# The filling of a softmax block moved behind the turning of its probabilities

## What is computed

```python
for i in range(S // Q_BLOCK):                       # 8 blocks of 128 queries
    s = einsum('bqhmd,bkhmd->bhmqk', q[:, q0:end], k[:, :end]) * scale   # m = 0, 1: two maps
    s = where(rel >= 0, s + bias, -inf)
    p = softmax(s, axis=-1)
    a = p[:, :, 0] - lam * p[:, :, 1]
    out = einsum('bhqk,bkhv->bqhv', a, v[:, :end])
```

## Time and profile before

| | |
|---|---|
| median of three runs | 2386.18 us (2385.57 to 2388.72) |
| the profiled execution | 2384.78 us, span in the trace 2383.0 us |
| TensorE (PE) busy | 2323.8 us, 98% of the span |
| VectorE (DVE) busy | 1611.8 us, 68% |
| ScalarE (ACT) busy | 990.7 us, 42% |
| GpSimd (POOL) busy | 298.8 us, 13% |
| chain that ended last | PE 87%, DVE 5%, DMA 2%, ACT 1% |

### The profile page before, as it was taken

The page is one execution under the profiler, slowest core; times in us unless marked ns, Lnnn a source line. Parts: engine busy times, 40 slices in busy tenths (PEclk is TensorE's granted clock), DMA queues, the critical chain, the costliest instruction groups (busy, mean ns, idle before and its releaser), DMA issues.

```text
span 2383.0 us, 30592 instructions
## 1 busy us (share of the span) xinstructions
PE 2323.8 (98%) x11354; PEld 1873.2 (79%) x11354; DVE 1611.8 (68%) x2740; ACT 990.7 (42%) x1891; POOL 298.8 (13%) x388
## 2 busy tenths in 40 slices
PE   7989999999999999999989999999999999999997
PEld 5778777788788888888778887777888888888886
DVE  6755677767877777576762556776687777655766
ACT  6422455544333233344753125555443333324454
POOL 0256400011000000220120110000200000003001
PEclk9999999999999999999999999999999999999999
DMA  8767501133454555662331111102324554227434
GB/s 306 254 240 225 164 18 35 55 107 92 156 171 151 196 171 150 181 207 95 127 122 45 39 34 45 28 27 80 115 71 168 186 198 173 80 71 240 145 104 153
DMA packets 216019, 311.29 MB, mean 131 GB/s; under 512 B 13207, under 2 KB 151368, under 8 KB 212928
## 3 DMA queue, kind: packets, MB, share of 16 engines
q1 hardware_dynamic: 182884, 188.31, 24.8%
q0 software_dynamic: 32528, 120.62, 15.1%
q10 hardware_dynamic: 460, 0.40, 0.1%
HBM read 243.48 MB, written 71.02 MB: 132 GB/s over the span
## 4 chain that ended last, share of the span: by engine, by line
PE 87%; DVE 5%; DMA 2%; issue 2%; ACT 1%; POOL 1%; SPq 1%; ACTq 0%; DVEq 0%; POOLq 0%
PE ps L3254 32%; PE ps L3293 15%; PE ps L2750 7%; PE ps L3134 7%; PE ps L2752 7%; PE ps L2751 7%; PE ps L3111 3%; PE ps L3080 3%; PE ps L2863 1%; PE ps L3099 1%; DVE ast L2088 1%; PE ps L2824 1%; PE ps L3062 1%; SPq L767 1%; DMA F<-in_w_down 1%
## 5 line engine op out<-in xcount | busy, mean ns | idle before, releaser
L3254 PE MATMUL ps<-hT,wsp 128*128 128x512 f32 x1440 | 333.5, 389 | 2.6 <-issue 2.6
L3254 PEld LDWEIGHTS ps<-hT,wsp 128*128 128x128 f32 x1440 | 269.9, 188 | 60.0 <-issue 4.0
L2750 PE MATMUL ps<-hT,wsp 128*128 128x512 f32 (+1 forms) x696 | 289.8, 416 | 0.0
L2752 PE MATMUL ps<-hT,wsp 128*128 128x512 f32 (+1 forms) x696 | 272.2, 391 | 0.0
L2751 PE MATMUL ps<-hT,wsp 128*128 128x512 f32 (+1 forms) x696 | 271.3, 390 | 0.0
L3293 PE MATMUL ps<-wsp,asp 128*128 128x512 f32 x1056 | 249.7, 392 | 0.2
L3293 PEld LDWEIGHTS ps<-wsp,asp 128*128 128x128 f32 x1056 | 198.1, 188 | 44.0 <-issue 1.0
L3254 PE MATMUL ps<-tsum,wasp 128*128 128x512 f32 x960 | 226.4, 392 | 0.3 <-DVE wasp L2544 0.3
L3254 PEld LDWEIGHTS ps<-tsum,wasp 128*128 128x128 f32 x960 | 180.2, 188 | 39.9 <-DVE wasp L2544 0.8
L2752 PEld LDWEIGHTS ps<-hT,wsp 128*128 128x128 f32 x696 | 131.5, 189 | 28.8
L2750 PEld LDWEIGHTS ps<-hT,wsp 128*128 128x128 f32 x696 | 131.8, 189 | 27.9 <-issue 7.3
(11 more groups left out here) (327 smaller groups left out, 4280.3 us busy)
## 6 DMA issues: line engine op xcount, KB each, us to landing
raw<-in_w_gate_up SPq DMA_DIRECT2D x48, 512.0 KB, 5.3
F<-in_w_mod SPq DMA_DIRECT2D x48, 512.0 KB, 5.5
raw<-in_w_in SPq DMA_DIRECT2D x45, 512.0 KB
raw<-sums_d SPq DMA_DIRECT2D x88, 256.0 KB, 3.0
F<-in_w_gate_up SPq DMA_DIRECT2D x40, 512.0 KB, 5.7
acts_d<-F POOLq DMA_DIRECT2D x38, 512.0 KB, 6.8
F<-acts_d POOLq DMA_DIRECT2D x76, 256.0 KB, 4.3
raw<-in_w_down SPq DMA_DIRECT2D x66, 256.0 KB, 4.0
```

Of the source, the lines that this page charges most:

```text
L2750: mm(o, a(0), b(0), start=start, stop=False)
L2752: return mm(o, a(1), b(0), start=False, stop=stop)
L3254: last = mm(bank(j, p), block_of(p, z)[:, k * P:k * P + P], times(p, zz, k), start=p < B_A22 and k == 0 and z == 0 and zz == 0, stop=k == ...
```

## The change

The two parts of the filling of a block are put together in one run that stands behind the turning of the block's probabilities (in block 7 ahead of the last tile, as the second part was). The number of steps of each block stays the same. `STEPS` holds one number a block, and the helper functions that find out which pieces and halves fall into a block give the same answer as before. The waits are those of the functions and move with them.

```diff
 EARLY = 4
-STEPS = (((2, 2), (2, 2), (3, 2), (2, 2), (2, 1), (2, 1), (2, 1), (1, 1)),
-         ((2, 2), (2, 2), (3, 2), (2, 2), (2, 2), (2, 2), (2, 2), (2, 1)),
-         ((2, 2), (2, 2), (3, 2), (2, 2), (2, 2), (2, 2), (2, 2), (2, 1)),
-         ((2, 2), (2, 2), (3, 2), (3, 2), (3, 2), (3, 2), (2, 2), (0, 0)))
+STEPS = ((4, 4, 5, 4, 3, 3, 3, 2), (4, 4, 5, 4, 4, 4, 4, 3), (4, 4, 5, 4, 4, 4, 4, 3),
+         (4, 4, 5, 5, 5, 5, 4, 0))
...
-                        a = NT * 16 + steps_before(h, b, 0)
+                        a = NT * 16 + steps_before(h, b)
                         if b:
                             weighted(h, b - 1)
-                        fill(a, a + STEPS[h][b][0])
                         if b == 0 and h:
                             weighted(h - 1, NT - 1)
                         turned(h, b, 0)
                         if b >= 4:
                             turned(h, b, 1)
-                        fill(a + STEPS[h][b][0], a + sum(STEPS[h][b]))
+                        fill(a, a + STEPS[h][b])
                         if h == HEADS - 1 and b == NT - 1:
                             out_first(0)
```

More of the change, by code:

```diff
@@ L120, with steps_before @@
 O_HOME = (2, 3, 0, 1, 6, 4, 5, 7)
-def steps_before(h, b, part):
-    return EARLY + sum(sum(p) for hh in range(h) for p in STEPS[hh]) + sum(
-        sum(p) for p in STEPS[h][:b]) + (STEPS[h][b][0] if part else 0)
+def steps_before(h, b):
+    return EARLY + sum(sum(STEPS[hh]) for hh in range(h)) + sum(STEPS[h][:b])
 def pieces_turned(h, b):
-    a = steps_before(h, b, 0)
-    return [i for i in range(len(PIECES)) if a <= 8 * i + 4 < a + sum(STEPS[h][b])]
+    a = steps_before(h, b)
+    return [i for i in range(len(PIECES)) if a <= 8 * i + 4 < a + STEPS[h][b]]
 def halves_ended(h, b):
-    a = steps_before(h, b, 0)
-    return range(a // 8, (a + sum(STEPS[h][b])) // 8)
+    a = steps_before(h, b)
+    return range(a // 8, (a + STEPS[h][b]) // 8)
 Y_PAIR = (0, 1, 2, 3, 0, 1, 0, 1)
```

## The result

The changed kernel takes 2394.8 us (median; 2394.3 to 2395.91) against 2386.11 us of the kernel before in the same comparison: 8.7 us more, a ratio of 1.0035 with a 95% interval of 1.0023 to 1.0047. The forecast was 2389.2 us with a range up to 2392.0 and no difference that can be measured as the likeliest. It was wrong; the kernel is slower, and by nearly three times the forecast.

What follows compares the result with a forecast made beforehand. The prediction took TensorE, busy 98% of the span, to bound the kernel. First-block waits of 1.65 + 1.39 + 0 gave +3.0 us on the median 2386.18, so 2389.2 us, with a range of 2385.5 to 2392.0.

Steps and rivals of the forecast that it cites:

- T(b) waits for the combination of block b: Every block: turning the probabilities waits for VectorE's scalar_tensor_tensor (line 2222); the first part of filling had covered this.
- T(7) waits in every head: Sign that the prediction is wrong: turning the probabilities of block 7 waits in every head.
- First blocks, 1.65 + 1.39 = 3.04: Head 0, block 0: turning waits for the combination, 1.65 us in layer 0 and 1.39 in layer 1.
- T(4) and T(5) eaten by S(6) and S(7): Head 0 block 4, heads 1 and 2 block 5: turning 0.28 and 0.03 us late, absorbed by later score waits; zero.
- T(1) covered in heads 1 to 3: Block 1, heads 1 to 3: 0.1 us left by old times, but exponentials come some 1.5 us sooner; covered.
- W(7) directly behind S(1), zero: Next head's first block: previous head's last weighted values follow scores directly; zero, bounded by 0.3 us six times, 1.7 us.
- pieces behind T, zero: The 12 pieces formerly turned in the first part of filling go at most 0.7 us later; zero.
- joints, zero: In 62 blocks, 0.08 us saved per second filling run cancels 0.08 lost by turning directly behind weighted values; zero.
- B: Rival: near misses bite in blocks 4, 5 and 7, and the last weighted values pay; +5.8, 2392.0 us; chance 0.17.
- D: Rival: granted clock halves behind first blocks' wait (+9.8, 2396.0) or in runs without filling (+30, 2416); chance 0.06, second way 0.02.
- Rival C: First-block delay partly given back at head 0's later score waits, 1.07 and 0.3 us a layer; +0.3, 2386.5; chance 0.13.
- Rival E: Faster: second filling runs saved, turning behind weighted values free, -2.0; old waits drained, another 4.2; 2380.0 us; chance 0.04.

Runs made afterwards that it cites:

- the step between: Changed kernel with one step of filling put between turned group 0 and group 1 in blocks 4 to 7: 2386.74 us, ratio 1.0006.
- the shorter copy: Changed kernel with ScalarE's two steps of outs turned round, copy out of PSUM first, then the square: 2391.29 us, ratio 1.0020.
- The mirror image: Kernel with blocks 4 to 7 of each head in the changed order, blocks 0 to 3 as before the change: 2393.39 us, ratio 1.0031.

## Why the prediction was wrong, by its own steps

- *"T(b) waits for the combination of block b"*, in the part on what bounds the kernel. This is the step that failed. It holds for group 0. Group 1 has a second input, the free bank, and the whole list of later blocks was worked out with the first input only. Missing term: 9 paid waits of 0.40 us a layer, 7.2 us in both, and 0.16 for block 5 of head 0. The row that named this wait was in the very view of the earlier trace rows, 0.2 us in the one block without filling, and was passed over as small. What shows once, where the cover is missing, is to be paid at each place where the cover is taken away, and at 0.40 us and not at the row's 0.2. One of the prediction's own signs of being wrong came true by this wait: T(7) waits in every head.
- *First blocks, 1.65 + 1.39 = 3.04.* Right mechanism; measured 1.27 and 1.28, in all 2.55. The start behind the end of a VectorE step was taken at 0.14 us and is 0.06 here (275.06 + 0.35 = 275.41, T(0) at 275.47, rows below): 0.16 in both layers. The 0.1 us for each wait that the prediction set beside this price does not show; the start came sooner than by the row, not later. The rest is mostly layer 0's chain, which is not tied to S(1): the combination ended 2.14 us behind the start of S(1) in the trace of before, 1.87 here, and 2.8 to 3.0 in four of the other traces.
- *T(4) and T(5) eaten by S(6) and S(7).* Right about what eats, wrong about what is eaten: T(4) came 0.11 late for its combination and T(5) not at all, this cost nothing, and what S(6) of head 0 (1.07 down to 0.67) and S(7) of heads 1 and 2 (0.39 down to none) took in was group 1's wait.
- *T(1) covered in heads 1 to 3; W(7) directly behind S(1), zero; pieces behind T, zero; joints, zero.* All right: blocks 0 to 3 of heads 1 to 3 became 0.1 us shorter in sum. These joints give back 0.3 to 0.4 us in a layer rather than nothing.
- *Sum.* Instead of 3.0: 2.55 + 7.2 + 0.16, less 0.8 of small gains, 9.1 in the traces of the heads; 8.7 in the medians.
- *Rivals B and D* came nearest in size (2392.0 and 2396.0 against 2394.8), by luck. B has blocks 4 to 7 right, but as late combinations. *Rival C* did not happen: head 0's S(6) kept waiting and the shift stayed. *Rival E* neither. The first way of D, a fall of the clock behind T(0)'s wait: not in the changed kernel, but once in another (last section). Its second way, scores, weighted values and transposes in one run with no filling, did not happen; here is the longest such run, block 6 of head 1, in a window of the changed kernel, 4.5 us at a clock of 1.00:

```profile
354.40:358.90 4.50, 4.31 (x28) 2.79 (x28) 3.98 (x8) 2.14 (x8) 0.00 (x0) 1.00 0.00 0
```

The Trainium skill, page "TensorE: Matmul & The Clock Gate", section "Part 4: PE-mode transpose", says that transposes don't count as busy for the clock as matmuls do. This trace neither bears it out nor refutes it: it shows only that seven transposes at the end of such a run left the clock at 1.00.

The first block of layer 0 in the changed kernel, TensorE and VectorE:

```profile
273.54 0.70 PE L3077 MATMUL ps<-F 64*128 64x256 f32 x4
...
275.06 0.35 DVE L2219 SCALAR_TENSOR_TENSOR F<-F,ast 128x128 f32<-128x128 f32 x1
...
275.47 0.33 PE L3096 MATMUL ps<-cst,F 128*128 128x128 f32 x1 [1.23 <-DVE F L2219]
```

## What to carry to other kernels

Before work is moved away from ahead of a step, list every semaphore that the step waits for, in each of its parts, and measure how long each has been ready, buffers that must come free among them; the input that the step is named after is only the first. A wait that shows once, small, at the one place without cover, will come at all the places where the cover goes. And where a bounding engine waits for chains of fixed length, count those waits first: they decide which new waits cost nothing, and moving independent work beside them was worth more here (5.5 us in either order) than the order (1 us at most).

## What the runs showed of the hardware

The first block of layer 0 was 1.27 us longer in the changed kernel, but 2.25 and 2.39 in the kernels with the step between and with the shorter copy, and 3.67 with blocks 4 to 7 undone, though all of them do the same there: the combination ended 1.9 to 3.0 us behind the start of S(1). The rows show two ways in which GpSimd makes it late. In the kernel with the shorter copy, GpSimd's step on line 922 stood behind the issue of a DMA, and VectorE, which takes its result ahead of the combination, waited for it:

```profile
272.73 0.72 POOL L978 DMA_DIRECT2D F<-in_w_down  x1 [4.17 <-DMA sums_d<-F]
...
273.46 1.07 POOL L922 TENSOR_TENSOR st<-st,mhalf 128x4 f32<-128x4 f32 x1
...
274.56 0.69 DVE L2145 TENSOR_TENSOR F<-ps,st 128x512 f32<-128x512 f32 x1 [1.08 <-POOL st L922]
```

With the step between, VectorE waited 0.94 us at the same place; in the changed kernel it did not wait there. With blocks 4 to 7 undone the combination itself met GpSimd, whose sums of weights start when a DMA has landed:

```profile
275.66 1.25 POOL L987 TENSOR_TENSOR F<-F 128x512 f32<-128x512 f32 x1 [1.14 <-DMA F<-in_w_down]
275.79 1.28 DVE L2219 SCALAR_TENSOR_TENSOR F<-F,ast 128x128 f32<-128x128 f32 x1
...
277.12 0.47 PE L3096 MATMUL ps<-cst,F 128*128 128x128 f32 x1 [2.16 <-DVE F L2219]
```

The scalar_tensor_tensor of 128x128 took 1.28 us beside GpSimd's tensor_tensor, against 0.35 alone, and ended 0.16 us behind it; TensorE waited 2.16 us. The mirror image shows it again, in the old order of this block:

```profile
274.40 1.44 DVE L2219 SCALAR_TENSOR_TENSOR F<-F,ast 128x128 f32<-128x128 f32 x1
274.41 1.28 POOL L987 TENSOR_TENSOR F<-F 128x512 f32<-128x512 f32 x1 [1.28 <-DMA F<-in_w_down]
...
275.90 0.33 PE L3096 MATMUL ps<-cst,F 128*128 128x128 f32 x1 [0.34 <-DVE F L2219]
```

With blocks 4 to 7 undone, the granted clock fell from 2.4 to 1.2 GHz at the end of that wait of 2.16 us, for 3.4 us (window of the same kernel):

```profile
276.90:280.30 3.40, 3.18 (x10) 2.77 (x11) 3.26 (x10) 1.30 (x5) 3.32 (x4) 0.50 0.35 103
```

Of the 3.67 us, 1.27 are the wait that the changed kernel has too and 0.93 the slower combination; 1.5 are left for the slower clock (half of the 3.4 us would be 1.7, an estimate). Waits of 2.22 and 2.36 us at the same place, in the other two kernels, left the clock at 1.00, so the length of the wait alone does not settle it; what does stays open. One profiled execution shows it, and whether it recurs in the same kernel was not tried. From the end of ScalarE's copy to the start of TensorE's matmul or weight load behind it there were 0.05 and 0.04 us in the rows above.
